# A two-block transformer on one core: gate and scale rows by DMA instead of by TensorE, low parts shared, transposes and a sum placed later

## The reference

```python
for layer in range(DEPTH):                                # 2
    mods = jnp.split(c_silu @ ada_w[layer] + ada_b[layer], N_MOD, axis=-1)   # 9 vectors of 1024
    sh, sc, g = mods[0], mods[1], mods[2]
    h = modulate(rms_norm(x, norm_g[layer, 0]), sh, sc)   # h * (1 + sc) + sh
    x = x + 0.5 * (1.0 + g) * swiglu(h, ffn_w_in[layer, 0], ffn_w_out[layer, 0])
    sh, sc, g = mods[3], mods[4], mods[5]
    h = modulate(rms_norm(x, norm_g[layer, 1]), sh, sc)
    y = pool_mixer(h, ...) if layer == 0 else moba_attention(...) @ w_o
    x = x + (1.0 + g) * y
    sh, sc, g = mods[6], mods[7], mods[8]
    h = modulate(rms_norm(x, norm_g[layer, 2]), sh, sc)
    x = x + 0.5 * (1.0 + g) * swiglu(h, ffn_w_in[layer, 1], ffn_w_out[layer, 1])
    if layer == 0:
        kv = shared_kv(x, ...)                            # keys (rope, norm) and values for layer 1
```

## Time and profile before

| | |
|---|---|
| median of 3 runs | 1231.69 us (1231.51 to 1232.03) |
| the profiled execution | 1231.7 us |
| its span, first to last instruction | 1229.9 us |
| busy, of the span | PE 97%, DVE 65%, ACT 48%, POOL 47% |
| mean granted TensorE clock | 0.996 of 2.4 GHz |
| moved by DMA | 293.18 MB, 238 GB/s on average |

### The profile page before, as it was taken

One profiled execution on the slowest core, in us unless ns is written; L12 is line 12 of the kernel. 1 busy time (PEld: TensorE's weight loads), 2 busy tenths in 40 slices (PEclk: granted clock), 3 DMA queues, 4 the chain that ended last, 5 costly groups with the idle time before them and its releaser, 6 DMA issues.

```text
span 1229.9 us, 15549 instructions
## 1 busy us (share of the span) xinstructions
PE 1198.4 (97%) x5816; PEld 984.1 (80%) x5816; DVE 805.2 (65%) x1115; ACT 592.0 (48%) x774; POOL 574.8 (47%) x420
## 2 busy tenths in 40 slices
PE   9999999999899999999999999999999999999998
PEld 6787887887678888778888888788888887888886
DVE  6885568845487778468778856697674665644432
ACT  6465564665543444454344356444342665534340
POOL 1455344654455435455453436764543463345360
PEclk9999999999899999999999999999999999999999
DMA  9976369835498988529989747799875434766550
GB/s 355 360 252 220 105 246 335 275 136 176 150 340 292 319 316 278 190 86 357 299 303 340 257 171 258 252 305 308 298 275 168 155 126 154 253 212 205 203 171 35
DMA packets 181657, 293.18 MB, mean 238 GB/s; under 512 B 8144, under 2 KB 99920, under 8 KB 181584
## 3 DMA queue, kind: packets, MB, share of 16 engines
q1 hardware_dynamic: 177552, 284.82, 67.6%
q10 hardware_dynamic: 4032, 7.38, 1.9%
HBM read 291.12 MB, written 1.05 MB: 238 GB/s over the span
## 4 chain that ended last, share of the span: by engine, by line
PE 84%; POOL 5%; DVE 5%; issue 3%; ACT 2%; DVEq 0%; ACTq 0%; POOLq 0%
PE ps L1770 49%; PE ps L1779 24%; PE ps L2042 2%; PE ps L1793 1%; POOL w_lo L496 1%; POOL stat L487 1%; PE ps L1858 1%; PE ps L1927 1%; PE ps L1943 1%; PE ps L1955 1%; ACT w_hi L626 1%; DVE x L1224 1%; PE ps L1900 1%; PE ps L1966 1%; PE ps L1915 1%
## 5 line engine op out<-in xcount | busy, mean ns | idle before, releaser
L496 POOL TENSOR_TENSOR w_lo<-raw,w_hi 128x512 fp32r<-128x512 f32 x352 | 492.9, 1434 | 449.2 <-ACT w_hi L626 449.2
L1770 PE MATMUL ps<-w_hi,h_hi 128*128 128x512 f32 x1120 | 444.8, 402 | 2.5 <-issue 1.4
L1770 PE MATMUL ps<-w_hi,h_lo 128*128 128x512 f32 x1120 | 433.1, 391 | 0.0
L626 ACT ACTIVATE w_hi<-raw 128x2048 fp32r<-128x2048 f32 x188 | 353.5, 1909 | 89.8 <-PE ps L1779 82.9
L1779 PE MATMUL ps<-w_lo,h_hi 128*128 128x512 f32 x1120 | 301.3, 391 | 3.8 <-POOL w_lo L496 2.0
L1128 DVE TENSOR_TENSOR w_lo<-raw,w_hi 128x2048 fp32r<-128x2048 f32 x96 | 228.0, 2379 | 100.9 <-ACT w_hi L626 100.2
L1770 PEld LDWEIGHTS ps<-w_hi,h_hi 128*128 128x128 f32 x1120 | 210.3, 188 | 52.0 <-issue 11.3
L1779 PEld LDWEIGHTS ps<-w_lo,h_hi 128*128 128x128 f32 x1120 | 210.0, 188 | 50.7 <-POOL w_lo L496 2.8
L1770 PEld LDWEIGHTS ps<-w_hi,h_lo 128*128 128x128 f32 x1120 | 211.2, 189 | 40.7
L1114 DVE SCALAR_TENSOR_TENSOR ps<-ada_raw,ccol,ps 128x512 f32<-128x512 f32 x240 | 181.0, 754 | 7.5 <-DMA ada_raw<-ada_w 0.3
L888 ACT ACTIVATE a_hi<-ps 128x512 fp32r<-128x512 f32 x44 | 26.3, 599 | 181.4 <-PE ps L2042 181.4
(11 more groups left out here) (194 smaller groups left out, 997.4 us busy)
## 6 DMA issues: line engine op xcount, KB each, us to landing
raw<-ffn_in SPq DMA_DIRECT2D x176, 512.0 KB, 5.5
ada_raw<-ada_w SPq DMA_DIRECT2D x144, 512.0 KB, 7.0
raw<-ffn_out SPq DMA_DIRECT2D x44, 1024.0 KB, 5.4
raw<-w_in SPq DMA_DIRECT2D x31, 1024.0 KB, 7.0
raw<-w_out SPq DMA_DIRECT2D x8, 1024.0 KB, 7.4
ada_raw<-kv_ada_w SPq DMA_DIRECT2D x16, 512.0 KB, 7.6
raw<-w_kv SPq DMA_DIRECT2D x8, 1024.0 KB, 5.5
bias<-na_bias ACTq DMA_DIRECT2D x16, 256.0 KB, 3.8
```

Source lines behind the costliest of these rows:

```text
L496: ins = pool.tensor_tensor(w_lo[:, u % RAW, piece], raw[:, u % RAW, piece], w_hi[:, u % RING, piece].bitcast(F32), ALU.subtract)
L626: act.activation(w_hi[:, u % RING, :], raw[:, u % RAW, :], ACT.Copy).then_inc(*S.inc("w_hi_ready", u))
L1770: pe.matmul(bank(b), part[:, k_in_lhs + k, tok], wh[:, k, c * 512:(c + 1) * 512], start=first_mm[c], stop=False)
```

## The change

1. The nine rows no longer come from PE and ACT. `row_store` (ACT's queue) writes a column vector of `mods` to a small DRAM tensor, `row_load` (ACT's queue) reads it back into all partitions, and the readers on DVE wait for `row_in`. In each `down` the store stands after the conversion of units 0 to 2 and the last activation group, the load after that of unit 4. The first `down` stores and loads `pool_scale`, `pool_shift` and `pool` there too. `final` is loaded from an input in row form at the end of the second encoder layer.
2. Units 1 and 2 of the first FFN's `up`, POOL's before, are shared between POOL and DVE; so is unit 2 of the last FFN's, DVE's before. The DVE halves are placed in `norm` and `final_update`.
3. `K_T`: key transposes of group 1 after step 23 instead of 20.
4. The sum whose last `ada` piece belongs to unit 8 goes one step later, from 14 to 15.

```diff
-K_MEAN, K_T = {7: 0, 12: 1}, {19: 0, 20: 1}
+K_MEAN, K_T = {7: 0, 12: 1}, {19: 0, 23: 1}
-POOL_UP_FIRST = {(0, 0): (1, 2), (0, 1): (1, 2)}
+POOL_UP_FIRST = {(0, 1): (1, 2)}
-            s = min(s for s in SUM_STEPS if s >= fill_step(e - first["in", layer]) + 2 and (layer, s) not in taken)
+            s = min(s for s in SUM_STEPS if s >= fill_step(e - first["in", layer]) + 2 + (e - first["in", layer] == 8) and (layer, s) not in taken)
+        ROWS = {("down", 0, 0): 2, "pool": 5, "pool_scale": 4, "pool_shift": 3, ("down", 0, 1): 8,
+                ("down", 1, 0): 13, "o": 16, ("down", 1, 1): 19}
+        mod_rows = nc.dram_tensor("mod_rows", (len(ROWS), D), F32, kind="Internal").ap()
-        shared_units = {first["in", 0], first["kv"] + 1, first["up", 1, 1] + 1, first["q"] + 1, first["q"] + 3}
+        shared_units = {first["in", 0], first["kv"] + 1, first["up", 1, 1] + 1, first["up", 1, 1] + 2,
+                        first["up", 0, 0] + 1, first["up", 0, 0] + 2, first["q"] + 1, first["q"] + 3}
 # POOL, norm(name, last), t == 0
                         low(last + 1)
                         low_first(last + 2)
+                        low_first(last + 3)
 # POOL, between the roots of tile 0 and tile 1 of fin and f00
-                    low(first["up", 0, 0] + 1)
-                    low(first["up", 0, 0] + 2)
+                    low_first(first["up", 0, 0] + 1)
+                    low_first(first["up", 0, 0] + 2)
 # ACT
-            def row_copy(name, into=row):
...
+            def row_store(name):
+                act.wait_ge(*S.at("mod_ready", ROWS[name]))
+                act.dma_start(row_of[name].rearrange("o (k p) -> p (o k)", p=P), mods[:, ROWS[name], :], allow_slow_non_contiguous=True).then_inc(
+                    row_out[name], 16)
+            def row_load(name, into=row):
+                act.wait_ge(row_out[name], 16)
+                act.dma_start(into[:], row_of[name].broadcast_to([P, D])).then_inc(row_in[name], 16)
 # ACT, end of the encoder layers
+                if layer == DEPTH - 1:
+                    act.dma_start(row[:], final_row.broadcast_to([P, D])).then_inc(row_in["final"], 16)
 # ACT, ffn
                 fill(d + 2)
                 high_act(NG - 1)
-                row_copy(("down", layer, i))
+                rows = [(("down", layer, i), row)]
+                if i == 0 and layer == 0:
+                    rows += [("pool_scale", pool_rows[:, 0, :]), ("pool_shift", pool_rows[:, 1, :]), ("pool", pool_gate)]
+                for name, _ in rows:
+                    row_store(name)
+                fill(d + 4)
+                for name, into in rows:
+                    row_load(name, into)
                 fill(d + NG - 1)
-            row_copy("pool", pool_gate)
-            row_copy("pool_scale", pool_rows[:, 0, :])
-            row_copy("pool_shift", pool_rows[:, 1, :])
 # ACT, attention
             mb_exps(0, 1, (2, 3))
+            row_store("o")
             fill(o + 3)
...
-            row_copy("o")
+            row_load("o")
 # DVE, norm
-                        lows(last + 2)
+                        lows(last + (3 if name == "f11" else 2))
...
                     stage_first(name, t, scale, shift)
+                    if name == "f00" and t == 0:
+                        lows(last + 2)
 # DVE, final_update
                 norm_mean("fin", t)
+                if t:
+                    lows(first["up", 0, 0] + 2)
 # PE: make_row and its nine calls go, for example
                     if n == 2:
-                        make_row(down, mods[:, gate_vec, :], [("mod_ready", gate_vec)])
```

More of the change, by code:

```diff
@@ L194, in program @@
             norm_cols, ada_b_cols, c_cols, na_bias, t5_bias, lam_rows, sub_cols, qk_rows,
-            pool_cols, rope, causal, window_weights, identity, out):
+            pool_cols, rope, causal, window_weights, identity, final_row, out):
     units, first = weight_units(w_in, w_out, ffn_in, ffn_out, pool_w, w_kv, w_q, w_o)
@@ L332, in program @@
         x_in_sem = [ctx.enter_context(nc.semaphore(f"x_loaded{t}")) for t in range(NT)]
+        ROWS = {("down", 0, 0): 2, "pool": 5, "pool_scale": 4, "pool_shift": 3, ("down", 0, 1): 8,
+                ("down", 1, 0): 13, "o": 16, ("down", 1, 1): 19}
+        mod_rows = nc.dram_tensor("mod_rows", (len(ROWS), D), F32, kind="Internal").ap()
+        row_of = {name: mod_rows[i:i + 1, :] for i, name in enumerate(ROWS)}
+        row_out = {name: ctx.enter_context(nc.semaphore(f"row_out{i}")) for i, name in enumerate(ROWS)}
+        row_in = {name: ctx.enter_context(nc.semaphore(f"row_in{i}")) for i, name in enumerate((*ROWS, "final"))}
         half_in = ctx.enter_context(nc.semaphore("first_half_loaded"))
@@ L840, in _ @@
             fill(first["up", 0, 0])
-            row_copy("final")
             squares_of_x = lg1.rearrange("p s t k -> p (s t k)")
@@ L1218, in update @@
                     if gate:
-                        for half in range(2):
-                            dve.wait_ge(*S.at("row_ready", gate, half))
+                        dve.wait_ge(row_in[gate], 16)
                         link(dve.tensor_tensor(bank(b, 2), bank(b, 2), gate_row[:], ALU.mult))
@@ L1445, in final_update @@
                 add_final(t)
-                for half in range(2):
-                    dve.wait_ge(*S.at("row_ready", "final", half))
+                dve.wait_ge(row_in["final"], 16)
                 dve.wait_ge(*S.at("x_ready", "fin", t))
@@ L1517, in gate01 @@
                 both = bank(acc_bank[("pool",), t], 2)
-                for half in range(2):
-                    dve.wait_ge(*S.at("row_ready", "pool", half))
+                dve.wait_ge(row_in["pool"], 16)
                 dve.tensor_tensor(both, both, pool_gate, ALU.mult).then_inc(*S.inc("gated01", t))
@@ L1530, in modulate_half @@
                 if t == 0:
-                    dve.wait_ge(*S.at("row_ready", "pool_scale", half))
-                    dve.wait_ge(*S.at("row_ready", "pool_shift", half))
+                    dve.wait_ge(row_in["pool_scale"], 16)
+                    dve.wait_ge(row_in["pool_shift"], 16)
                 link(dve.scalar_tensor_tensor(out=hn[:, t, c], in0=x[:, t, c], scalar=st(t), in1=pool_rows[:, 0, c],
@@ L1891, in mix_across @@
                     mix_part(half, 1, 0)
[L1893 to L1902, removed]
             def encoder_work(layer, s):
@@ L2014, in _ @@
                     row_pair_half(out_name, 4, i, t, (yn_hi, yn_lo) if half else (h_hi, h_lo), b, 2 * (i % 2))
-                    if s == 3 and layer == DEPTH - 1:
-                        make_row("final", gcols[:, 2, :])
                     if s == 6:
@@ L2056, in after_down @@
                         actT(NG - 1)
-                    if n == 2:
-                        make_row(down, mods[:, gate_vec, :], [("mod_ready", gate_vec)])
[L2059 to L2064, removed]
                 column_product(name, NG, h_ready(norm_name), lambda g: ("act_ready", name, g), after_up)
@@ L2184, in _ @@
             queries_T(1, 1)
-            make_row("o", mods[:, 16, :], [("mod_ready", 16)])
             mb_pT(1, 0)
@@ L2284 @@
         "window_weights": window_weights(),
-        "identity": np.eye(P, dtype=f32),
+        "identity": np.eye(P, dtype=f32), "final_row": get("final_g").reshape(1, D),
     }
```

## The result

The changed kernel takes **1253.4 us** (median of 4 executions, 1246.5 to 1255.3) against 1231.9 us for the kernel before on the same chip: 1.6% slower, ratio 1.0162, interval 1.0122 to 1.0201. The forecast was 1214.7. It went the way of the second rival, which had 10%.

A forecast was written before the change was run, and what follows sets the result against it. PE, busy 97% of the span, was taken to bound the kernel; 7.6 (rows) + 1.1 (bank wait) + 1.3 (sum) + 1.6 (keys) + 5.4 (first norm) = 17.0 us off 1231.7 gave 1214.7 us, range 1211 to 1229.

The forecast's parts named there:

- second rival: First `down`: element stores take part in the weights' turns, ACT is freed at 504, a 34 us stall; 1248.7 us, chance 12%.
- Stores "in time: cost 0": First `down`: four element stores land in 8 + 2 us, before ACT must be free at 470.5; cost 0, ends 0 and 34.
- threshold for "slower": First `down`: the change loses once ACT is free later than 487.5, that is from 0.12 us per 4-byte packet.
- The end of 34 us: First `down`: the upper end of the stores' cost, where ACT waiting for them stalls the kernel by 34 us.
- An issue takes 0.33 us: ACT's queue: each row store or load takes 0.33 us to issue, and ACT has that time since `row_copy` is gone.
- The clock: First FFN's norm: with less idle time PE's granted clock stays at 1.00 instead of falling to 0.50; 2.8 us gained.
- Rival 1: First `down`: rows late, still faster; ACT free at 481.7, 11.2 us of stall, 14 with the clock; 1228.7 us, chance 22%.
- Rows off PE, 7.6 + 1.1: Nine rows' transposes leave PE, row "o" counted half: 7.6 us; the bank wait before the pool_scale row goes: 1.1 us.
- Sum and keys, 1.3 + 1.6: PE's waits go before the sum moved to step 15, 1.3 us, and before group 1's later key transposes, 1.6 us.
- First norm, 5.4: First FFN's norm: shared low parts bring its chain 2.9 us earlier, -0.3 for DVE's half, 2.8 for the clock.
- Last norm, 0: Last FFN's norm: the low-part wait only moves to the transposes, behind a root beside DVE's low part; 0 us.
- rival 3: FFN norms: DVE holds up POOL's pieces and the clock falls, 2.6 to 4.3 us less gain; 1217.5 to 1222 us, chance 10%.

The follow-up runs named there:

- runs_of_32: The changed kernel with column blocks stored as they lie in SBUF, 128 runs of 32 bytes instead of 1,024 of 4 (values in another order): 1218.0 us.
- others_alone: The kernel before with only the shared low parts at two FFN norms, the later sum and the later key transposes; rows still made by PE: 1225.1 us.
- rows_T: The changed kernel with column blocks turned by a PE transpose and stored as 512-byte runs; row `o` back on PE: 1218.8 us.
- root_first: The kernel before with all edits but the rows, and DVE waiting for the first FFN norm's second root before its next low part: 1223.3 us.
- sum_and_keys: The kernel before with only the sum a step later and the key transposes three steps later: 1229.9 us, ratio 0.9972.
- rows_alone: The kernel before with the rows by DMA as the only edit: 1259.4 us, ratio 1.0216.
- late_loads: The changed kernel with the row loads, and ACT's wait for the stores, behind the last weight conversion of each `down`: 1234.0 us.

## Why the prediction was wrong, point by point

- **Stores "in time: cost 0"**: the step that failed. I took 30 ns for a 4-byte packet, a third of the queue's mean packet of the earlier trace rows. A store has 64 such writes for each of 16 engines, so its 9.4 us are 147 ns a write until it has landed, and the four together 45.9 us / 256 = 179 ns. My own threshold for "slower" was 120 ns. The packet was not the wrong part: it takes 11 ns, even less than my 30. What was wrong is the step from the packet's time to the landing, and that the weights would go on beside it. The end of 34 us is near the 34.4 us that the stores cost by runs_of_32, but that is luck: rival 2 had ACT free at 504 and 34 us of idle time; ACT was free at 495.4, PE idle for 24.1 us, and the slower clock made up most of the rest. What misled me was that I argued from bytes and from the queue's mean packet of 1,830 bytes, which says nothing of when an element write lands, and that I held the weights' turns to be protected. The rule of "DMA: Bandwidth & Descriptors" in the Trainium skill that the prediction weighed, a descriptor for every element, spoke for the bad end. The same page, "Back-pressure in remote DMA", says that stalled writes stall a DMA engine's other queues too; it speaks of another transfer, but the 36 GB/s agree with it.
- **"An issue takes 0.33 us"**: true of one store (0.38 median), not of four: 22.67 us. I had no such hold on the list. So the first late weights were those of the fourth unit, before the wait that I had watched.
- **The clock** fell with the stall (0.50 in 470 to 480), 8.5 us of the first FFN's 32.6. Rival 1 had put 2.8 on this, rival 2 nothing.
- **Rows off PE, 7.6 + 1.1**: right in kind, and within the noise in size. From others_alone to runs_of_32, 7.1 us (4.5 to 9.7). The bank wait before a row went with the rows, as argued: it is in others_alone (1.07 us) and not in rows_T.
- **Sum and keys, 1.3 + 1.6**: right (3.4 measured for 2.9), neither wait is left.
- **First norm, 5.4**: too much. Idle time before the transposes fell by 3.0 (1.44 + 4.02 to 2.42), for the 2.9 forecast. The new wait behind DVE's half of unit 1 is 1.2 us where I had 0.3, because that half takes 2.16 us beside POOL's pair instead of 1.22. And the clock's 2.8 came back only in part: transposes to the next low group took 5.2 us before (323.53 to 328.71), 4.3 in others_alone (320.19 to 324.44), 2.8 in root_first (318.19 to 320.97). So 3.0 - 1.2 + 0.9 = 2.7 us; others_alone against sum_and_keys gives 3.8 (1.5 to 6.1). Idle for 2.42 us here the clock fell, idle for 2.27 us in the pooling it stayed: my reading between two rows was too fine. It may not even fall each time: two of others_alone's four executions took 1226.3 and 1227.0 us with a mean granted clock of 0.996, the other two 1223.9 with 0.999.
- **Last norm, 0**: the number is right, the account only in part. The wait for unit 2's low part did go, but it did not join the one before the transposes: DVE's half of unit 1, now beside two more pieces of POOL, takes 2.35 us where it took 1.23, and PE waits 1.48 us for it. In all 1.48 + 1.01 us against 0.36 + 1.46 + 0.41. Nor does the root stand beside DVE's low part any more: it takes 0.56 us (2.54 before).
- **Sum**: with harmless stores the change gives 14.4 us (runs_of_32) where I had 17.0. Without the one step the forecast would have been 2.6 off. Two ends in the prediction do not follow from its terms, and nothing hangs on them: rival 3's "2.6 to 4.3 us less" gives 1217.3 to 1219.0 and not 1222, and its own range's 1211.5 lies below what the upper ends of the terms reach (some 1213).

## What to carry to other kernels

Price a transfer by its number of writes and their length and not by its bytes: 4 KB blocks turned by one transpose into runs of 512 bytes cost next to nothing here, and as 1,024 elements each they hold up the weights, whether or not anyone waits for them. Do not put such stores on the queue of an engine that feeds the critical one, and never several at once; whether another engine's queue would have spared the weights, no run shows. A small engine instruction in a chain (a root on one column) is worth a wait by the other engine that would run beside it.

## What was unexpected of the hardware

- Issuing element stores behind each other can hold the issuing engine: of eight issues the median is 0.38 us, and the fourth in a row takes 18.88. With half the writes the four took 2.96 us instead of 22.67.
- The DMA engines show 0.98 busy while they move 106 GB/s, and 0.79 at 36: the busy share does not tell starved weights from flowing ones, the GB/s do. The busy time is that of the weights' own packets, drawn out from 117 to 535 ns, while the 4-byte packets take 11 ns each.
- Runs of 32 bytes are no worse than runs of 512 by these times: 1218.0 against 1218.8 us, though the latter kernel also has four transposes and row `o` on PE. From 4 to 8 to 32 bytes the median landing goes 15.3, 5.9, 4.0 us.
- Executions with element stores scatter: the change 1246.5 to 1255.3, rows_alone 1251.7 to 1266.1, late_loads 1230.2 to 1245.5; runs_of_32 stays within 0.9 us.
